# Where the third and fourth weight units of an output projection are split, and where decays are clipped

## What is computed

```
decay = exp(gc[l] - gc[s])          (0 above the diagonal)
T = inverse(I + strict(kb k^T * decay))
v_new = T v - (T k) S;   o = q S + (q k^T * decay) v_new;   S = S * gl + k_dec^T v_new
out = rms_norm(x + gate * ((rms_norm(o) * silu(z)) @ gdn_w_out))
```

## Time and profile before

| | us |
|---|---|
| median of 3 runs | 1071.32 (1071.28 to 1071.86) |
| the profiled execution, its own time | 1063.69 |
| its span | 1061.6 |
| TensorE (PE) busy in it | 1024.1 |
| VectorE (DVE) busy | 658.7 |
| ScalarE (ACT) busy | 436.1 |
| GpSimd (POOL) busy | 221.6 |
| granted TensorE clock, mean | 0.995 |

### The profile page before, as it was taken

The page is one execution under the profiler, slowest core; times in us unless marked ns, Lnnn a source line. Parts: engine busy times, 40 slices in busy tenths (PEclk is TensorE's granted clock), DMA queues, the critical chain, the costliest instruction groups (busy, mean ns, idle before and its releaser), DMA issues. The chain is left out here.

```text
span 1061.6 us, 14031 instructions
## 1 busy us (share of the span) xinstructions
PE 1024.1 (96%) x5374; PEld 831.3 (78%) x5374; DVE 658.7 (62%) x1077; ACT 436.1 (41%) x868; POOL 221.6 (21%) x168
## 2 busy tenths in 40 slices
PE   9999999999999999999899999999999898989997
PEld 5888888888766677788688788878888677878886
DVE  4245656621257668758646667774796877976736
ACT  4223234332458843332434333365433447224432
POOL 0010000000001342104000001100106753046792
PEclk9999999999999999999899999999999999999999
DMA  8277642234232343231524437335412122203502
GB/s 312 80 254 240 236 136 85 90 111 147 89 87 75 116 158 93 94 121 40 171 78 159 157 136 263 120 124 175 176 63 100 44 96 80 80 23 118 179 2 80
DMA packets 60818, 132.35 MB, mean 125 GB/s; under 512 B 6096, under 2 KB 6480, under 8 KB 60624
## 3 DMA queue, kind: packets, MB, share of 16 engines
q1 hardware_dynamic: 58304, 118.67, 33.2%
q0 software_dynamic: 2304, 12.58, 3.3%
q10 hardware_dynamic: 144, 0.20, 0.1%
HBM read 117.22 MB, written 14.22 MB: 124 GB/s over the span
## 5 line engine op out<-in xcount | busy, mean ns | idle before, releaser
L285 DVE TENSOR_TENSOR w_lo<-raw,w_hi 128x2048 fp32r<-128x2048 f32 x57 | 134.2, 2355 | 215.4 <-ACT w_hi L281 199.3
L281 ACT ACTIVATE w_hi<-raw 128x2048 fp32r<-128x2048 f32 x51 | 97.4, 1912 | 200.6 <-PE projections_ps L126 156.9
L124 PE MATMUL projections_ps<-projections_x_hi,w_hi 128*128 128x512 f32 x208 | 81.1, 390 | 0.4 <-ACTq L641 0.4
L125 PE MATMUL projections_ps<-projections_x_lo,w_hi 128*128 128x512 f32 x208 | 80.9, 389 | 0.0
L126 PE MATMUL projections_ps<-projections_x_hi,w_lo 128*128 128x512 f32 x208 | 80.9, 389 | 0.0
L124 PE MATMUL projections_ps<-w_hi,projections_x_hi 128*128 128x512 f32 x192 | 74.9, 390 | 0.0
L126 PE MATMUL projections_ps<-w_hi,projections_x_lo 128*128 128x512 f32 x192 | 74.7, 389 | 0.0
L125 PE MATMUL projections_ps<-w_lo,projections_x_hi 128*128 128x512 f32 x192 | 74.7, 389 | 0.0
L242 DVE SCALAR_TENSOR_TENSOR resid<-resid,mixer_cw 128x512 f32<-128x512 f32 x96 | 64.9, 746 | 0.0
L748 POOL TENSOR_TENSOR tok<-tok,attention_recip 128x512 f32<-128x512 f32 x8 | 8.3, 1042 | 231.0 <-DVE attention_recip L836 231.0
L124 PE MATMUL mixer_ps<-w_hi,mixer_ha_hi 128*128 128x512 f32 (+1 forms) x132 | 53.0, 402 | 2.6 <-DVE mixer_ha_lo L3038 1.3
(11 more groups left out here) (359 smaller groups left out, 2477.2 us busy)
## 6 DMA issues: line engine op xcount, KB each, us to landing
raw<-in_w_in SPq DMA_DIRECT2D x26, 1024.0 KB, 5.0
raw<-in_gdn_w_in SPq DMA_DIRECT2D x24, 1024.0 KB, 5.0
tok<-in_ada_w POOLq DMA_DIRECT2D x16, 768.0 KB, 6.3
raw<-in_w_out SPq DMA_DIRECT2D x8, 1024.0 KB, 5.0
qkv_kept<-mixer_ring SPq DMA_DIRECT2D x8, 1024.0 KB, 4.2
mixer_st<-qkv_kept SPq DMA_DIRECT2D x32, 256.0 KB, 3.0
raw<-in_gdn_w_out SPq DMA_DIRECT2D x8, 1024.0 KB, 5.5
resid<-in_att_bias SPq DMA_DIRECT2D x16, 256.0 KB, 2.7
```

The costliest lines, as they stand in the source:

```text
L124: nc.tensor.matmul(out, w_hi, x_hi, start=first, stop=False, skip_group_check=True)
L125: nc.tensor.matmul(out, w_hi, x_lo, start=False, stop=False, skip_group_check=True)
L281: self.nc.scalar.activation(self.hi[s][:], self.raw[s][:], ACT.Copy).then_inc(self.hi_ready, 1)
L285: engine.tensor_tensor(self.lo[s][:], self.raw[s][:], self.hi[s][:], ALU.subtract)\
```

## The change

1. First mixer: the two clips of L710 go from ScalarE to VectorE, after the attention loop. All four later tiles are turned and rounded before the first group; all four `att_square` come before `copies(1)`. GpSimd sets its constant earlier and makes the row factor before `skip(1)`.
2. Second mixer, output units: unit 2 gets a slot of its own made of the staging buffers. It is loaded into `raw0`, rounded into `raw1` by ScalarE at slot (3, 5) of the first scan (when the last v is turned), and GpSimd makes its rest in place in `raw0` after `begin(1)`. Unit 3 is loaded into `w_lo0` when unit 0 is used up (`yp_half` 1), rounded into `w_hi0`, its rest made in place by VectorE before step 17 of the inversion. Units 4 and 5 change slots. `stage_v(1, 0)` and the load of unit 4 wait for `yp_half` 2.
3. Clips of half 1 move from slots (1, 2), (1, 6), (2, 2), (2, 14) to (1, 10), (2, 14), (2, 15), (3, 13); exponentials from (1, 15), (2, 2), (2, 15), (3, 6) to (2, 2), (3, 6), (3, 13), (3, 15). The fourth `log_decay_steps` goes from j = 2 to j = 3. `select(1)` goes from slot (3, 5) and `select_decays(1)` from ahead of `tokens_of(1, 0)`, both to behind `tokens_of(1, 1)`.

```diff
+            as_split = [views.enter_context(nc.sbuf_tensor(f"raw_split{i}", [P, HALF, COLS], F32R)) for i in range(2)]
...
+            as_raw = views.enter_context(nc.sbuf_tensor("w_lo_raw", [P, HALF, COLS], F32))
...
-            for s in range(SSM_GROUPS):
-                act.wait_ge(steps_ok, s + 1)
-                nc.scalar.activation(steps_in[:, s], steps_in[:, s], ACT.Relu).then_inc(first_clipped, 1)
...
-            for e in range(4, 7):
+            for e in range(4, 8):
                 high(e)
             decay(1)
-            att_square(0)
-            high(7)
-            att_square(1)
+            for t in range(TT):
+                att_square(t)
             copies(1)
-            for t in range(2, TT):
-                att_square(t)
...
+            for s in range(SSM_GROUPS):
+                dve.wait_ge(steps_ok, s + 1)
+                nc.vector.tensor_scalar(steps_in[:, s], steps_in[:, s], 0.0, None, ALU.max).then_inc(first_clipped, 1)
             for e in range(2):
                 low(e)
...
-            for e in range(4, 7):
+            for e in range(4, 8):
                 turn_m(e)
             group(0, (0,))
-            turn_m(7)
             steps_ahead(1)
...
+            nc.gpsimd.memset(half_neg[:], -0.5).then_inc(pool_step, 1)
             for s in range(STEPS):
-                skip(s)
                 if s == 1:
                     pool.wait_ge(sum_ok, TT)
-                    nc.gpsimd.memset(half_neg[:], -0.5).then_inc(pool_step, 1)
                     rsqrt(att_f[:], att_f[:], ALPHA ** 2 / D_MODEL, ALPHA ** 2 * EPS1)
+                skip(s)
...
-        OUT_UNITS = ((0, 0, 0, 0), (1, 0, 4, 0), (0, 0, 0, 1), (1, 1, 4, 1),
-                     (0, 0, 8, 0), (1, 0, 12, 0), (0, 0, 8, 1), (2, 1, 12, 1))
+        OUT_UNITS = ((0, 0, 0, 0), (1, 0, 4, 0), (3, 0, 0, 1), (0, 2, 4, 1),
+                     (1, 0, 8, 0), (0, 0, 12, 0), (1, 0, 8, 1), (2, 1, 12, 1))
+        OUT_HI = [w.hi[0][:], w.hi[1][:], w3[0][:], as_split[1][:]]
+        OUT_LO = [w.lo[0][:], w.lo[1][:], w3[1][:], as_split[0][:]]
+        OUT_RAW = [raw[0][:], raw[1][:], as_raw[:]]
...
+        def rest_made(queue, v):
+            queue.wait_ge(wo_lo[OUT_UNITS[v][0]], out_count(v, 0))
...
-        CLIPS_AT = [(1, 2), (1, 6), (2, 2), (2, 14)]
-        EXPS_AT = [(1, 15), (2, 2), (2, 15)]
+        CLIPS_AT = [(1, 10), (2, 14), (2, 15), (3, 13)]
+        EXPS_AT = [(2, 2), (3, 6), (3, 13), (3, 15)]
...
             load_out(2)
-            sp.wait_ge(vt_made, at(0, 1, 3, 1))
-            load_out(3)
...
-            sp.wait_ge(wo_lo[0], 2)
-            load_out(4)
             sp.wait_ge(kk_made, at(1, 1, 3, 1))
             stage(1, 1)
-            sp.wait_ge(wo_lo[1], 2)
+            sp.wait_ge(yp_half, 1)
+            load_out(3)
+            sp.wait_ge(yp_half, 2)
             stage_v(1, 0)
+            load_out(4)
...
-                    evacuate_y(0)
-                    evacuate_y(1)
-                    round_out(2, yp_half, 1)
-                    evacuate_y(2)
-                    evacuate_y(3)
-                    round_out(3, yp_made, TT)
+                    for u in range(4):
+                        evacuate_y(u)
+                    round_out(3, yp_half, 1)
                     evacuate_y(4)
                     evacuate_y(5)
-                    round_out(4, yp_half, 2)
+                    round_out(4, yp_made, TT)
...
+                        if i == 0 and (j, n) == (3, 5):
+                            round_out(2, vt_made, HB)
...
-                    if i == 0 and j in (1, 2):
-                        log_decay_steps(1, j + 1)
+                    if i == 0 and j in (1, 3):
+                        log_decay_steps(1, 2 + j // 2)
...
                 if i == 0:
                     begin(1)
+                    out_rest(nc.gpsimd, pool, 2)
...
                     tokens_of(i, j)
+                    if i and j == 1:
+                        select(1)
+                        select_decays(1)
                     decayed(i, j)
...
-                    invert_32(i, {9: lambda: out_rest(nc.vector, dve, 2), 16: lambda: out_rest(nc.vector, dve, 3)})
+                    invert_32(i, {17: lambda: out_rest(nc.vector, dve, 3)})
...
-                        elif i == 0 and n == 5:
-                            select(1)
```

More of the change, by code:

```diff
@@ L147, in build @@
         gain = sb("gain", [P, KT])
+        with ExitStack() as views:
+            as_split = [views.enter_context(nc.sbuf_tensor(f"raw_split{i}", [P, HALF, COLS], F32R)) for i in range(2)]
+            for i in range(2):
+                views.enter_context(nc.sbuf_tensor(f"below_raw{i}", [P, HALF, COLS], F32))
+            as_raw = views.enter_context(nc.sbuf_tensor("w_lo_raw", [P, HALF, COLS], F32))
         raw = [sb(f"raw{i}", [P, HALF, COLS]) for i in range(2)]
@@ L172, in build @@
                                       pool_dmas, logs, logs_t, logs_kept, steps_in, logs_in, heads, wba, wba_in, att_f, row_f, modc, g_col, gain)
-        second_mixer(nc, a, cleared, ahead, wba, wba_in, split, raw, masks, resid, row_f, modc, gain, small, tok)
+        second_mixer(nc, a, cleared, ahead, wba, wba_in, split, raw, as_split, as_raw, masks, resid, row_f, modc, gain, small, tok)
 def spare_buffers(resid):
@@ L1649, in scan_and_output, with second_mixer @@
         return sync, tensor, scalar, gpsimd, vector
-def second_mixer(nc, a, cleared, ahead, wba, wba_in, split, raw, masks, resid, row_f, modc, gain, small, z):
+def second_mixer(nc, a, cleared, ahead, wba, wba_in, split, raw, as_split, as_raw, masks, resid, row_f, modc, gain, small, z):
     w_in = a["gdn_w_in"][0].rearrange("(k p) c -> p k c", p=P)
@@ L1821, in second_mixer @@
         m_turned, m_hi_ok, m_lo_ok = sem("m_turned"), sem("m_hi_ok"), sem("m_lo_ok")
-        wo_in = [sem(f"wo_in{r}") for r in range(2)]
+        wo_in = [sem(f"wo_in{r}") for r in range(3)]
         wo_hi = sem("wo_hi")
-        wo_lo = [sem(f"wo_lo{s}") for s in range(3)]
+        wo_lo = [sem(f"wo_lo{s}") for s in range(4)]
         yp_half, yp_made, yp_out = sem("yp_half"), sem("yp_made"), sem("yp_out")
@@ L1850, in out_rest @@
             queue.wait_ge(wo_hi, v + 1)
-            engine.tensor_tensor(OUT_LO[slot][:], raw[r][:], OUT_HI[slot][:], ALU.subtract).then_inc(wo_lo[slot], 1)
+            engine.tensor_tensor(OUT_LO[slot], OUT_RAW[r], OUT_HI[slot], ALU.subtract).then_inc(wo_lo[slot], 1)
+        def rest_made(queue, v):
+            queue.wait_ge(wo_lo[OUT_UNITS[v][0]], out_count(v, 0))
         def at(i, per_head, j, k):
@@ L2260, in y_triple @@
                     if t == 0:
-                        pe.wait_ge(wo_lo[half], n + 1)
+                        rest_made(pe, 2 * n + half)
                 if v == 0 and half == 0:
                     pe.wait_ge(m_lo_ok, kk + 1)
+                slot = OUT_UNITS[2 * n + half][0]
                 mm = three_products(nc, ps[:, Y_BANKS[v], :], m_hi[:, k, rows_t], m_lo[:, k, rows_t],
-                                    w.hi[half][:, kk, :], w.lo[half][:, kk, :], k == 0, k == KT - 1)
+                                    OUT_HI[slot][:, kk, :], OUT_LO[slot][:, kk, :], k == 0, k == KT - 1)
                 if kk == HALF - 1:
@@ L2562, in round_out @@
                 act.wait_ge(done, count)
-                nc.scalar.activation(OUT_HI[slot][:], raw[r][:], ACT.Copy).then_inc(wo_hi, 1)
+                nc.scalar.activation(OUT_HI[slot], OUT_RAW[r], ACT.Copy).then_inc(wo_hi, 1)
             def evacuate_y(u):
@@ L2670, in fill @@
                                 gate_out_half(0)
-                        elif i == 0 and n == 6:
-                            exps(1, 3)
                         elif i == 0 and n == 11:
@@ L2677, in fill @@
                             gate_out_half(1)
+                        if i == 0 and (j, n) == (3, 5):
+                            round_out(2, vt_made, HB)
+                        if i == 0 and (j, n) in EXPS_AT:
+                            exps(1, EXPS_AT.index((j, n)))
                     for c in range(TT):
@@ L3041, in heads_of @@
             def heads_of(i):
-                select_decays(i)
+                if i == 0:
+                    select_decays(0)
                 for j in range(HB):
@@ L3070, in fill @@
                                 doubled(i, j + 1, *part_at(j + 1, n))
-                            if i == 0 and (j, n) in CLIPS_AT:
-                                clip(1, CLIPS_AT.index((j, n)))
                         elif n in (3, 4, 6, 8):
@@ L3082, in fill @@
                                 .then_inc(gate_in, 1)
+                        if i == 0 and (j, n) in CLIPS_AT:
+                            clip(1, CLIPS_AT.index((j, n)))
                     for c in range(TT):
```

18 lines of the change are left out of this document (7 added, 11 removed).

## The result

| | before | after |
|---|---|---|
| median | 1071.33 (4 runs, 1071.28 to 1071.86) | 1055.35 (4 runs, 1055.09 to 1055.80) |
| profiled execution, own time | 1063.69 | 1055.48 |
| its span | 1061.6 | 1053.5 |
| its mean granted TensorE clock | 0.995 | 0.997 |

The ratio of the medians is 0.985, with a 95% interval of 0.9833 to 0.9867: 16.0 us less. The two profiled executions differ by 8.2 us, against a sum of 8.0.

The account below looks back on a forecast made before the run. TensorE, busy 1024.1 of 1061.6 us, was taken as the bound, with VectorE's order making its gaps. Terms summed to -8.0: profiled 1063.69 to 1055.7, plus 7.6 carried to the median, 1063.3; range 1061.0 to 1067.0.

Parts of the forecast that it names:

- first mixer's clips on VectorE: First mixer, window 357 to 368: two clips leave ScalarE, which runs 2 us earlier; -1.0 (bounds 0 and -1.04).
- last tile turned with the others: First mixer, first group: the 0.89 gap waiting for that tile's low part goes; -0.9.
- squares before copies(1), factor earlier: First mixer: copies(1) moves back 2.3 us, the factor comes about 3 earlier, the 0.87 gap stays; 0 (-0.87 to +1.4).
- clips out of (1, 2), (1, 6): Second mixer: emptying both slots removes TensorE's gaps of 0.57 and 1.81; -2.4.
- clip at (1, 10): Second mixer: the clip waits for GpSimd's expansion and delays the sum, so L2205 starts later; +0.8 (0 to 1.3).
- clip out of (2, 2), table load there: Second mixer: emptied slot wins -2.7; ScalarE's first exponential with its table load landing there costs +0.2 (0 to 1.28).
- clip at (3, 13): Second mixer: a clip ahead of the scan's last sum, with a little waiting for GpSimd; +0.5 (0 to 4.5).
- one split out of the inversion: Inversion: one VectorE split leaves the chain, TensorE waits 1.0 instead of 3.19; -2.2 (0 to -2.3).
- Rival 1: Second mixer: clips meet GpSimd again, at (3, 13) VectorE waits up to 4.5; total -4.0, 1067.3; chance 0.10.
- Rival 2: First mixer gains nothing: squares hold copies(1), the gain is lost at the next group; total -6.1, 1065.2; chance 0.10.
- Rival 3: Inversion: unit 3's load comes late, VectorE waits 2.4 in the chain; total -5.6, 1065.7; chance 0.05.
- Rival 4: Second mixer: another link holds the inversion, clips only trade places; -1.9 alone, 1069.4; chance 0.06.

## Why the prediction was wrong, step by step

**The step that failed** is the one that stood behind the sum: "The runs' median is 1071.32, 7.6 above the profiled one; I carry the difference over unchanged". The 7.6 were not a constant of the measurement. They are time at half of TensorE's clock, behind waits that the change removes, and the one profiled execution had none of it. The larger part is the long stretch: 17.1 us in the second trace of the kernel before, 13.7 in that of the first mixer alone, and by time and clock in 63 of 90 runs of the kernel before. The wait of 1.81 at (1, 6) precedes it. So the edit whose wait I priced at 1.8 was worth 6 to 9 in the median: moving that clip alone, with a wait of 0.5 in its new place, gave 6.0, and putting it back cost 8.9. The smaller part is the short stretch, 3.4 to 6.8 us in four traces, at the inversion's wait of 3.19, which the change brings to 1.12. An estimate from the medians: 6.0 less 1.3 of waiting is 4.7 for the first; the split put back cost 1059.99 - 1055.35 = 4.6, less 2.0 of waiting is 2.6 for the second; together 7.3 of the 7.6. The two views that hinted at it were both read: the profile's mean clock of 0.995 beside a time 7.6 below the median, and three waits of 1.81 to 3.19 in the stretches that the change touches. That the three runs of before agreed within 0.6 us made the difference look like a constant; ten runs on each of five chips show two bands.

The Trainium skill describes such falls in the page TensorE: Matmul & The Clock Gate, section "HAM oscillation — how this bites in real kernels": there, waits of TensorE (for DMA, some 3 to 5 us each) make its clock fall again and again, and the products after each run slow. The runs here agree in kind, at shorter waits, of 1.18 to 1.91 us at (1, 6) and (2, 6), with 5 to 8 us lost; they disagree with any rule by the length of the wait alone, since 2.72 at (2, 2) cost 0.7 more than itself in one trace and nothing more in another.

**The terms of the sum**, as the two profiled executions show them:

| term | forecast | measured | from |
|---|---|---|---|
| first mixer's clips on VectorE | -1.0 | -0.8 | idle in 357 to 368: 1.04 to 0.25 |
| last tile turned with the others | -0.9 | -0.9 | the 0.89 is gone |
| squares before copies(1), factor earlier | 0 | +0.4 | 0.87 to 1.23 |
| clips out of (1, 2), (1, 6) | -2.4 | -2.4 | both gaps gone |
| clip at (1, 10) | +0.8 | +0.5 | 0.51 |
| clip out of (2, 2), table load there | -2.5 | -2.7 | no gap left |
| clip at (2, 15) | +0.7 | +0.6 | 0.61 |
| select(1) away | -1.0 | -0.8 | 1.05 to 0.22 |
| clip at (3, 13) | +0.5 | +0.2 | 0.67 (in front of L2134) to 0.90 |
| one split out of the inversion | -2.2 | -2.1 | 3.19 to 1.12 |
| sum | -8.0 | -8.0 | span: 1061.6 - 1053.5 = 8.1 |

The gap of 0.67 ahead of L2134, which the sum used without a row, is that at 879.00 in the trace of before.

That 8.1 stands against 8.0 is in part luck, as the starts of the same products in the two traces show: the changed kernel is 0.7 later at 20 us and again wins 0.7 at 508, where the lower clock lasts 3.4 us instead of 6.8; the change touches neither place, and the two cancel. Between them and behind, it wins 1.7 in the first mixer (forecast 1.9), 4.3 in the scan of half 0 (forecast 3.9) and 2.1 at the inversion (forecast 2.2).

**Rival 1**, clips that meet GpSimd: none did; all four took 1.21 to 1.24. My 873.0 and 877.1 for the split and the clip at (3, 13) were counted in the times of before; here everything is 6.1 earlier (L2134 at 872.88 instead of 879.00), so they stand for 866.9 and 871.0. Measured are 865.96 and 871.13: in place of an overlap of 0.4 a distance of 0.63. That the rival was real is shown by the clip at (3, 7), 2.33, and the one put back at (1, 6), 2.14. **Rival 2**, the first mixer gains nothing: its mechanism is there and smaller. VectorE waits 3.05 for `copies(1)`, and the gap grew by 0.4 instead of 1.9, as `masked(1)` ended at 380.8 and not at the 380.0 that I put; the first mixer's part alone gave 1.3 in its trace and 2.0 in the lowest runs. With `copies(1)` two squares earlier the 1.23 shrank to 0.43, which shows the cause, and 0.72 came back 30 us on. **Rival 3**, unit 3 late: its load took 4.9 and the rounding ended 1.5 before it was needed; I had said 1.6. **Rival 4** falls: the inversion's wait went by 2.07, and it returns to 3.13 with the split. None of the four, and nothing in my range beyond 2.3 us, had a gain larger than the sum.

The drain behind a table load that the Trainium skill gives (ScalarE: Activation LUTs, "What ACT_TABLE_LOAD costs"), by which a term would have been +1.6, is not seen after the change either: the load runs from 841.19 to 842.47, the exponential starts at 842.48, and no gap of TensorE stands near (2, 2). The Trainium skill's rule that a VectorE instruction with two SBUF inputs and a GpSimd instruction that reads SBUF exclude each other (SBUF — State Buffer, "Who interferes with whom") agrees with the clips of 2.14, 2.33 and 3.73 against 1.21.

## What to carry to other kernels

When a profiled execution and the median of the runs differ by much more than the runs among themselves, compare the mean granted clock first: the trace in hand may lack what the median contains, and a change to its waits moves that too. A wait of TensorE over 1 us in a stretch of small products cost several times its length here in the clock behind it, so look at such a wait before three of 0.5. Gaps of 0.5 to 1.2 at boundaries with the same next engine were for the most part given back at the next one; two attempts on 1.1 to 2.3 us of them won 0.6 to 0.7 in the traces and nothing that the medians tell.

## What was not expected of the hardware

- The same program, with the same wait of 1.81 us, ran the 17 us behind it at 0.50 of the clock in one profiled execution and at 1.00 in the other; by times and clocks 63 of 90 executions are of the first kind, and 5 to 8 us of the whole hang on it.
- At (1, 6) a wait of 1.18 was followed by it in 3 runs of 10, one of 1.71 in 9 of 10; at (2, 6) one of 1.91 in ten runs of 10; at (1, 2) one of 1.69 in none of 4; at (2, 2) one of 2.72 by 3.4 us in one trace and by none in two; at the end of the inversion one of 3.07 to 3.19 by 3.4 to 6.8 us in four traces of seven. (Where runs are counted, it is by their times and clocks.) Why the places differ is open.
- While the clock was at 0.50 TensorE was busy without a gap (4.00 of 4.00 in each window), and the level came back after 13.6 to 17.1 us, with TensorE busy all along.
